# Where the columns of shift and scale are summed: between the seventh and the eighth output tile instead of inside the norm

## The reference

```python
mod = silu(c) @ ada_w[i] + ada_b[i]          # 3 x 1024: shift, scale, gate
h = rmsnorm(x, norm_g[i]) * (1 + scale) + shift
x = x + gate * mixer(h)                      # mixer = (...) @ w_out
```

## Time and profile before

| | us |
|---|---|
| median of 3 runs | 3030.13 |
| lowest and highest run | 3028.6 and 3041.08 |
| the profiled execution's own time | 3021.97 |
| its span | 3020.0 |
| TensorE busy (matmuls) | 2838.9 |
| VectorE busy | 1318.2 |
| GpSimd busy | 1069.3 |
| ScalarE busy | 668.7 |

### The profile page before, as it was taken

One profiled execution on the slowest core, in us unless ns is written; L12 is line 12 of the kernel. 1 busy time (PEld: TensorE's weight loads), 2 busy tenths in 40 slices (PEclk: granted clock), 3 DMA queues, 4 the chain that ended last, 5 costly groups with the idle time before them and its releaser, 6 DMA issues.

```text
span 3020.0 us, 33392 instructions
## 1 busy us (share of the span) xinstructions
PE 2838.9 (94%) x12155; PEld 1882.9 (62%) x12155; DVE 1318.2 (44%) x2682; ACT 668.7 (22%) x1588; POOL 1069.3 (35%) x574
## 2 busy tenths in 40 slices
PE   6899999999999998998889978999999999999997
PEld 5465544475555544654657546588888544788886
DVE  6233365315555622335544165444365321433464
ACT  2132134223333412323323122111100100211101
POOL 4783484088470018706820000386000583000000
PEclk7999999989999999998888989999999999999998
DMA  7342342253331023323210100254322453222222
GB/s 237 116 127 82 108 126 77 84 157 98 85 91 35 29 89 117 108 77 86 87 39 25 59 0 27 92 162 125 95 80 88 126 164 100 70 83 88 93 82 72
DMA packets 244979, 278.26 MB, mean 92 GB/s; under 512 B 39251, under 2 KB 217696, under 8 KB 244736
## 3 DMA queue, kind: packets, MB, share of 16 engines
q1 hardware_dynamic: 215872, 175.56, 19.1%
q0 software_dynamic: 28224, 100.86, 10.8%
q10 hardware_dynamic: 768, 0.30, 0.0%
HBM read 274.59 MB, written 2.10 MB: 92 GB/s over the span
## 4 chain that ended last, share of the span: by engine, by line
PE 84%; DVE 5%; DMA 4%; issue 2%; ACT 2%; POOL 1%; SPq 1%; DVEq 0%; ACTq 0%; POOLq 0%
PE psum L709 26%; PE psum L1340 24%; PE psum L887 11%; PE psum L873 3%; PE psum L736 3%; PE psum L861 3%; PE psum L1167 2%; PE psum L1215 2%; PE psum L769 2%; PE psum L1185 1%; DMA ring<-in_ffn_w_up 1%; PE psum L1015 1%; PE psum L1016 1%; DMA ring<-in_ffn_w_gate 1%; PE psum L1307 1%
## 5 line engine op out<-in xcount | busy, mean ns | idle before, releaser
L709 PE MATMUL psum<-h,ring 128*128 128x512 f32 (+1 forms) x1808 | 767.4, 582 | 13.3 <-ACT h L1562 6.4
L636 POOL DMA_DIRECT2D ada_ring<-in_ada_w x192 | 114.7, 597 | 1429.7 <-DVEq L2101 952.4
L709 PEld LDWEIGHTS psum<-h,ring 128*128 128x128 f32 x1808 | 341.6, 192 | 400.0 <-issue 388.2
L648 POOL TENSOR_SCALAR ada_ring<-ada_ring,cond 128x1024 f32<-128x1024 f32 x168 | 480.4, 2859 | 8.5 <-POOL ada_sum L652 1.8
L652 POOL TENSOR_TENSOR ada_sum<-ada_sum,ada_ring 128x1024 f32<-128x1024 f32 x168 | 396.0, 2357 | 14.9
L887 PE MATMUL psum<-og,ring 128*128 128x512 f32 x768 | 333.3, 593 | 2.3 <-DVE og L2636 2.0
L1340 PE MATMUL psum<-og,arena 128*128 128x256 f32 x1152 | 258.6, 379 | 1.7 <-ACT probs L1913 1.7
L887 PEld LDWEIGHTS psum<-og,ring 128*128 128x128 f32 x768 | 144.6, 190 | 182.2 <-issue 178.7
L1340 PEld LDWEIGHTS psum<-og,arena 128*128 128x128 f32 x1152 | 218.7, 190 | 32.1 <-issue 2.4
L1340 PE MATMUL psum<-h,ring 128*128 128x256 f32 x768 | 178.4, 383 | 1.6 <-issue 0.8
L1586 ACT ACTIVATE psum<-psum,neg_max 128x256 f32<-128x256 f32 (+4 forms) x288 | 150.1, 521 | 109.2 <-DVE neg_max L2186 83.0
(11 more groups left out here) (332 smaller groups left out, 3783.9 us busy)
## 6 DMA issues: line engine op xcount, KB each, us to landing
ada_ring<-in_ada_w POOLq DMA_DIRECT2D x192, 512.0 KB, 4.0
ring<-in_ffn_w_gate SPq DMA_DIRECT2D x22, 1024.0 KB, 5.3
ring<-in_ffn_w_up SPq DMA_DIRECT2D x22, 1024.0 KB, 5.4
ring<-in_ffn_w_down SPq DMA_DIRECT2D x16, 1024.0 KB, 5.1
ring<-in_sc_w_in SPq DMA_DIRECT2D x12, 1024.0 KB, 5.4
ring<-in_mla_w_in SPq DMA_DIRECT2D x10, 1024.0 KB, 6.0
ring<-in_mla_w_out SPq DMA_DIRECT2D x8, 1024.0 KB, 5.1
ring<-in_swa_w_in SPq DMA_DIRECT2D x16, 512.0 KB, 5.4
```

The source lines that it names most:

```text
L636: pool.dma_start(ada_ring[:, i % 2, :], w[k * P:(k + 1) * P, first(part)]).then_inc(arrived[i % 2], n.give(f"ada_in{i % 2}", 16))
L648: step = nc.gpsimd.tensor_scalar(piece, ada_ring[:, i % 2, :], c, None, ALU.mult)
L709: m = pe.matmul(tile.at[:, part], lhs(k), rhs(k), start=(k == 0), stop=(k == K - 1))
```

## The change

The sixteen columns of shift and scale are summed in one piece, into a tile of their own, between the seventh output tile and the eighth, in all six borders behind an output projection. `result_squares` is then called with `summed=True` and holds only the squares' sums, the spread and the gate's columns. VectorE calls `border_columns` in `add_result`, ahead of the eighth tile, instead of behind the reciprocal; ScalarE skips the columns' tile there, and one tile fewer behind the squares. In the border of the feed-forward stage (job 7) the place stays, but all sixteen columns now stand ahead of the wait for the last square; VectorE still takes them behind the reciprocal (`if job == 7`). The gate's columns stay where they were. The tile order changes with it: the eighth output tile takes the bank of the seventh, and the columns take the one between.

```diff
+            def border_columns(job):
+                pe.wait_ge(S["ada_step"], (1 + job * PARTS - (job >= CTX_JOB)) * KT)
+                column_sums(next_tile(), range(16), True)
+
-            def result_squares(job, frees_slot=False):
+            def result_squares(job, frees_slot=False, summed=False):
                 pe.wait_ge(S["sum_step"], n.take("sum_step", KT - 2))
                 added = token_sums(SB[0], sq_sum, True, False)
                 if frees_slot:
                     added.then_inc(S["slot_begun"], n.give("slot_begun"))
-                if job is not None:
-                    pe.wait_ge(S["ada_step"], (1 + job * PARTS - (job >= CTX_JOB)) * KT)
-                    tile = next_tile()
-                    column_sums(tile, range(8), False)
+                if job is not None and not summed:
+                    border_columns(job)
                 pe.wait_ge(S["sq_ready"], n.take("sq_ready"))
                 token_sums(SB[0], sq[:, 1, :], False, True).then_inc(S["sum_done"], 1)
                 if job is not None:
-                    column_sums(tile, range(8, 16), True)
                     spread_inverse()
...
                 for c in range(2, KT):
+                    if c == KT - 1:
+                        border_columns(job)
                     out_part(c, range(KT))
-                result_squares(job)
+                result_squares(job, summed=True)
...
                 for c in range(2, KT):
+                    if c == KT - 1:
+                        border_columns(job)
                     out_part(c, range(KT))
-                result_squares(job, frees_slot=True)
+                result_squares(job, frees_slot=True, summed=True)
...
                     else:
+                        if c == KT - 1 and columns:
+                            skip(1)
                         evacuated(next_tile())
...
             squares_of_result()
-            skip(2)
+            skip(1)
             shift(1)
...
             def normed(job, source=None, part=slice(0, T), inv=RB, columns=None):
 
-                if columns is not None:
+                if job == 7:
                     border_columns(*columns)
...
             def final_norm(g, columns=None):
 
                 give_inverse()
-                if columns is not None:
-                    border_columns(*columns)
...
-            def add_result(job, before_last=None):
+            def add_result(job, columns, before_last=None):
...
                 for c in range(KT):
+                    if c == KT - 1:
+                        border_columns(*columns)
                     tile = next_tile()
                     done(tile)
...
-            add_result(0)
+            add_result(0, (1, col("norm_g", 8, 8)))
             give_inverse()
             normed(1, columns=(1, col("norm_g", 8, 8)))
```

More of the change, by code:

```diff
@@ L1612, in attention_counts, with squares_of_result, squares_of_x @@
                 return {k: len(units) for k in ("nbias_ready", "exp_done", "probsT_done", "probsT_ready")}
-            def squares_of_result(added=None):
+            def squares_of_result(added=None, columns=True):
                 nc.scalar.activation(table_load[:, :], C["eps"], ACT.Sqrt)
-                squares_of_x(added)
+                squares_of_x(added, columns)
                 root_of_squares()
-            def squares_of_x(added=None):
+            def squares_of_x(added=None, columns=False):
                 steps = n.of["sum_step"].at
@@ L1996, in _ @@
             squares_of_result()
-            skip(1)
             shift(3)
@@ L2807, in block2_vector @@
                 state_space()
-                add_result(5, lambda: first_weights_of(7))
+                add_result(5, (6, col("norm_ffn_2", 0, 8)), lambda: first_weights_of(7))
                 give_inverse()
@@ L2814, in block2_vector @@
                 short_convolution()
-                add_result(7, lambda: first_weights_of(None))
+                add_result(7, (8, col("norm_ffn_2", 8, 8)), lambda: first_weights_of(None))
                 give_inverse()
@@ L2879, in _ @@
             swa()
-            add_result(1)
+            add_result(1, (2, col("norm_g", 16, 8)))
             give_inverse()
@@ L2883, in _ @@
             nsa()
-            add_result(2)
+            add_result(2, (4, col("norm_mix_2", 0, 8)))
             give_inverse()
@@ L2887, in _ @@
             mla(1)
-            add_result(3)
+            add_result(3, (5, col("norm_mix_2", 0, 8)))
             final_norm(col("final_norm_g", 0, 8), (5, col("norm_mix_2", 0, 8)))
```

## The result

The changed kernel takes 3055.89 us (median of 4 runs, 3053.85 to 3066.69) against 3031.27 (4 runs, 3028.6 to 3041.08): ratio 1.0086, 95% interval 1.0068 to 1.0104, about 25 us slower. Measured twice more on other occasions it stood at 1.0061 (1.0043 to 1.0079) and 1.0088 (1.0069 to 1.0107). The mean of the three, 1.0078, is 24 us.

What follows compares the result with a forecast made beforehand. TensorE's own work, without waits in the borders, was taken as the bound. Six borders at +2.73 (+16.4), the feed-forward border's +1.6 and the clock's +4.5 gave +22.5 us on the 3030.13 median: 3052.6 us, range 3039 to 3063.

Steps and rivals of the forecast that it cites:

- Columns ahead of the eighth tile, +3.57 us each: Six projection borders: sixteen column sums ahead of the eighth output tile lengthen TensorE's stream by 3.57 us, 0.223 a column.
- The spread 0.84 us earlier: Six projection borders: without column sums ahead, the last square's sums and then the spread of the inverse start 0.84 us earlier.
- The feed-forward border, +1.56 us: Border behind the first feed-forward stage: eight more columns ahead of the last square's sums delay the spread by 1.56 us.
- Edits at no cost: VectorE's moved border operations, the bank swap, the wait for GpSimd's sums, SyncE's transfers and ScalarE's count: all covered, costing nothing.
- The serial sum, +18.0 us: Whole kernel without the clock: six projection borders, together +16.4 us, plus the feed-forward border's 1.6, make +18.0 us.
- The clock, +4.5 us as three borders at 1.5: Two new waits per projection border: three of six borders lose about 1.5 us to TensorE's lower clock, +4.5 us.
- the last border's 1.00: Row at 2995 us: the kernel's last border, with the new wait pattern, kept full granted clock until 3000.5.
- the rival without any fall: Six projection borders: the clock never falls, so only the serial +18.0 us, 3048 us; chance 0.16.
- The skill's rule: TensorE's clock falls back only over one long idle gap; neither new wait would do it, sum stays 18.0 us.
- the columns hide under the products: Rival, out projection: weight loads hide under long products, sixteen columns take 1.4 us, total 3033 us; chance 0.07.
- the delay is taken up later: Rival, after the borders: shrinking waits for weights or GpSimd return 4 to 8 us, 3040 to 3044; chance 0.12.
- it falls in every border: Rival, six projection borders: the clock falls in all, 10 us, total +28 us, 3058 us; chance 0.10.

Runs made afterwards that it cites:

- experiment 3: Repeat measurements against the kernel before: changed kernel with fillers in the six borders' two new waits, ratio 1.0057; changed kernel a third time, 1.0088.
- experiment 7: Changed kernel with one column of ones instead of 128 as moving operand of the sixteen columns' sums; ratio 1.0117 to the kernel before.
- experiments 6 and 7: Changed kernel with the six borders' sixteen columns summed twice, 1.0159; changed kernel with one moving column of ones instead of 128, 1.0117; both against the kernel before.
- experiment 9: Kernel before with feed-forward columns placed in its waits and unread matmuls in long waits of hybrid and state-space stages; 3022.95 against 3032.14 us, ratio 0.9964.

## Why the prediction was right

- **Columns ahead of the eighth tile, +3.57 us each.** The block measures 3.57 us in the chain; doubled it takes 7.15.
- **The spread 0.84 us earlier.** It came 3.67 us behind the sums instead of 4.48, 0.81. At the next product it is 0.88 in the three borders ahead of a mixer of the first block (6.52 against 7.40) and 0.79 in the two of the second block (7.05 against 7.84); the border ahead of the final norm has 0.80 at its spread. Net for a border +2.69 to +2.78 against the +2.73 forecast.
- **The feed-forward border, +1.56 us.** It is +1.55.
- **Edits at no cost.** VectorE's border operations were done 6.4 us ahead of the eighth tile's end in the first block and 5.2 us in the second. The block began without a gap behind the seventh tile, and the eighth tile 3.57 us behind the block's start, in all six borders, so neither GpSimd's sums nor the bank kept TensorE waiting.
- **The serial sum, +18.0 us.** 6 x 3.57 less 3 x 0.88, 0.80 and 2 x 0.79 is 16.4, with 1.55 it is 17.95. The kernel with fillers, which keeps the waits and takes away only their effect on the clock, measured +17.3, give or take 4.
- **The clock, +4.5 us as three borders at 1.5.** In the borders it was three or four at mostly 1.4 to 1.6 us, as forecast. In the total it is the softest term and stays so: falls in the borders can take the place of falls elsewhere (experiment 3), and the total saw between nothing and 6 us of them. That three falls were assumed was a choice between none and all six, and the row that spoke against more, the last border's 1.00, was a window that ended 0.4 us too early. So the forecast had the mechanism right at the border, and its agreement in the total, +22.5 against +24.6, is partly luck: on one occasion the changed kernel stood 18.6 us above the one before, the value of the rival without any fall.
- **The skill's rule.** The Trainium skill (TensorE: Matmul & The Clock Gate, section "HAM oscillation") speaks of a single long gap. Here two waits of 1.28 and 1.54 us with a short burst between them were enough, and in experiment 7 a stretch without any wait.
- **Rivals.** That the columns hide under the products was refuted twice (experiments 6 and 7). That the delay is taken up later was not seen: the kernel with fillers keeps 17.3 of 18.0 us, though a return of some 4 us could not be told from none. That the clock never falls in the borders is refuted by the three traces. That it falls in every border happened in none of them.

The total forecast was +22.5 us, measured +24.6 at first and 24 in the mean of three ratios. The 18 us of serial work are well founded; the 6 us above them are as uncertain as the clock term.

## What to carry to other kernels

Work that an engine has to do anyway is free only where that engine waits. Before moving it off the critical chain, ask whose chain it is: here the norm's latency looked like the path, but TensorE's own work filled it to the last tenth of a microsecond, so each column taken out of a wait bought an idle TensorE and cost its full 0.223 us elsewhere. Write down the length of each wait (here 1.28 and 1.55 us) and give it work of that length; a wait left empty can cost a second time through the clock. Matmuls that nobody reads took some 10 us back in the long waits of experiment 9; in the short waits of the borders they kept the clock, but what that is worth in the total is not settled. And when a row is read as proof that something does not happen, look also at what comes just behind it.

## What the hardware showed that I had not expected

- Two waits of 1.28 and 1.54 us within 3.3 us brought the lower clock level (1.2 GHz) in 11 of the 18 projection borders of three traces, at 1.4 to 1.6 us each in most and 2.4 to 2.5 us in two; fillers brought that to none of the 12 in both traces of that kernel.
- A fall is not tied to its place: the same wait of 2.02 us was followed by the lower level in the changed kernel (at 372.9) and not in the kernel before, and where the last projection border lost the clock, the fall 37 us behind it, which most other traces have, was missing.
- A block of 32 matmuls with a one-column output ran without a gap, and the clock fell behind or within it in five of six projection borders of that trace; in the three traces of the changed kernel, with 128 columns, it did so in none of 18.
- A column's sum took the same 0.11 us a record with one moving column as with 128.
